# Branch gates and branch projections with tokens as output rows, in a two-block float32 kernel on one core

## The chip, the cores and the metric

The kernel runs on one core of a Trainium2 chip. TensorE, VectorE, ScalarE, GpSimd and the DMA queues each run their own program and meet at semaphores. The metric is the device time of one execution in microseconds, the median of several runs. All data are float32.

## What is computed

Two blocks of a sequence model over 256 tokens of width 1024. The change touches the middle of the first one:

```python
h = _rmsnorm(x, norm_mix_g[l])
z = h @ w_in[l]
(hq, hf, hi, hg, fq, fk, fv, ff, mq, gate_logits) = jnp.split(z, pts, axis=-1)
y_a = _hgrn2_mixer(...)      # 256 x 512
y_b = _fox_mixer(...)        # 256 x 512
y_c = _memory_mixer(...)     # 256 x 512
gates = jax.nn.sigmoid(gate_logits).reshape(B, T, N_BRANCH, D_MODEL)
merged = (gates[:, :, 0] * (y_a @ w_br_hgrn[l])
          + gates[:, :, 1] * (y_b @ w_br_fox[l])
          + gates[:, :, 2] * (y_c @ w_br_mem[l]))
x = x + merged @ w_out[l]
```

`gate_logits` is 256 x 3072; each branch projection is 512 x 1024, `w_out` 1024 x 1024. Feed-forward layers, a second attention block and more feed-forward layers follow.

## The kernel before

**Split precision.** Each matrix product is made of three float32r products on TensorE: high parts times high parts, high times low, low times high (`three`, L379). Weights come from memory in units of 128 x 2048, numbered in the order of use (`weight_plan`, `U[key]`). SyncE loads a unit into one of three raw buffers, ScalarE writes its high part `wh` (`hi_to`, L1039), VectorE subtracts it for the low part `wl` (`lo_to`, L1483). There are three slots of each, so unit j can't have its high part made before TensorE is done with unit j - 3 (`unit_end`). Both helpers are called by the other two programs at places written out by hand; `begin(key)` brings the parts up to two units ahead of the key's own. Each engine works strictly through its own list.

**Gates.** There are twelve gate units `("gate", u)` of 256 columns. `rows_out` (L421) makes one: the weights are the stationary operand, the turned activations `hT` (256 tokens wide) move, so the output has features as rows and tokens as columns: 2 x 8 x 3 matmuls of 256 columns. The PSUM banks are 0, 1, 6, 7 in turn for the first eight units, and 0 and 1 for the last four. VectorE multiplies the bank with the per-token norm factor into `BIGT` (`rows_scaled`, L1577). Between the units TensorE does the small products of the recurrent branch (`own_products`, `level_products`, `cross_products`, `hgrn_out`), for which VectorE and ScalarE prepare operands in the same loop over u (L1178, L1746). In iteration 7 ScalarE also places blocks into `Am` (L1187) and takes the sigmoid of the first eight gate units in four pieces (L1167); from iteration 8 an exponential is needed again (L1193), and each change between sigmoid and exponential loads a table.

**Branches.** `branch(bi, u, half, ...)` (L811) makes a quarter of a branch's projection: 24 matmuls of 256 columns, features as rows. VectorE multiplies it with its gate in `BIGT` (`gated`, L1854). GpSimd adds branches 0 and 1, VectorE adds branch 2 into `merged` and counts `mrg_all`. As `merged` has features as rows, ScalarE copies its high part (`merged_hi`) and VectorE its low part (`merged_lo`) straight from SBUF into `yTh`, `hTh`, `yTl`, `hTl`, where they are the stationary operand of the output projection (`stretch`, L881; units `("wo", 1, c, r)`). In VectorE's list the low part of the second of these units comes last, in two halves around `merged_lo(3)`.

**The form with tokens as rows** exists already: `toks_halves` (L475) takes two row halves of a 512-column weight unit; for each half r and each token half m, the activations are stationary and 512 columns of weights move, 12 matmuls into one bank per m. `hg`, `hi` and `mv` use it, and ScalarE evicts them with `half_scaled` (L1084), where the norm factor is a scale per partition.

Of the kernel before, what the change touches and what calls it, by code (L numbers as in the profile page):

```python
# [5 lines left out]
F32 = mybir.dt.float32  # L6
# [92 lines left out]
def weight_plan(I):  # L99
# [5 lines left out]
    plan += row_halves("hi", w_in, 1024)  # L105
    plan += [(("gate", u), cols(w_in, 4104 + 256 * u)) for u in range(12)]
    for u in range(2):
# [27 lines left out]
def build(nc, plan, I, out):  # L135
    ctx = ExitStack()
    with ctx:
# [79 lines left out]

        mrg_fox, mrg_all, m_hi, m_lo = (sem(n) for n in ("mrg_fox", "mrg_all", "m_hi", "m_lo"))

# [67 lines left out]
        def emptied(key):  # L287
            return ps_free[at[key][0]], 1

        def raw_ready(i):  # L290
# [75 lines left out]
        def pe_program(pe):  # L366
# [303 lines left out]

            for u in range(12):
                rows_out(("gate", u), WF if u < 8 else W, mid=cross_products if u == 10 else None)
                if u == 0:
                    own_products()
                elif u < 8:
                    level_products(u - 1)
                elif u == 10:
                    hgrn_out()

            b = T.take()  # L680
# [129 lines left out]

            def branch(bi, u, half, src, ready=None):  # L811
                i, b = U["br", bi, u], W.take()
                t = take(("br", bi, u, half), b)
                if half == 0:
                    weights(i)
                for m in range(2):
                    o = (2 * half + m) * 128
                    ins = three(t[:, m * 256:m * 256 + 256], weight_left(i, 512, o), right(src), EIGHT[:4], True, True,
                                ready if m == 0 else None)
                ins.then_inc(ps_full[b], 1)  # L820
                unit_end[i] = full(("br", bi, u, half))

# [48 lines left out]
            branch(1, 1, 1, hT_at)  # L871
            for u in range(2):
                for half in range(2):
                    branch(2, u, half, hT_c, (lambda k: free(("mo", k // 2)) if k % 2 == 0 else None) if (u, half) == (0, 0) else None)

# [28 lines left out]
            weights(U["wo", 1, 1, 0])  # L904
            pe.wait_ge(m_lo, 2)
            for m in range(2):
                stretch(("wo", 1, 1, 0), ts[m], m, EIGHT[:4])
            weights(U["wo", 1, 1, 1])
            for n, ks in enumerate(((4, 5), (6, 7))):
                pe.wait_ge(m_lo, 3 + n)  # L910
                for m in range(2):
                    stretch(("wo", 1, 1, 1), ts[m], m, ks)
# [122 lines left out]
        def act_program(act):  # L1035
# [119 lines left out]
            for m in range(2):  # L1155
                half_scaled(Iv, "hi", m, rs0)
            begin(("gate", 0))

# [5 lines left out]
            def gate_sigmoid(j):  # L1164
                g = BIGT[:, j * 1024:j * 1024 + 1024]
                act.wait_ge(*free(("gate", 2 * j + 1)))
                act.activation(g, g, ACT.Sigmoid).then_inc(gate_sig, 1)  # L1167

            def mem_squares(half):
                act.wait_ge(mem_in, 16)  # L1170
                for m in range(2):
                    if half or m:
                        act.wait_ge(mem_sq, 2 * half + m)
                    act.activation(Vm[:, 0:512], Hn[:, m * 1024 + half * 512:m * 1024 + half * 512 + 512], ACT.Square,
                                   accum_out=mstat[0][:, 2 * half + m:2 * half + m + 1]).then_inc(mem_sq, 1)

            level(0)
            for u in range(12):  # L1178
                begin(("gate", u))
                if u in (5, 6):  # L1180
                    mem_squares(u - 5)
                if 1 <= u <= 6:
                    level(u)
                elif u == 7:
                    act.wait_ge(*free(("lv", 4)))
                    for x in range(0, 128, 32):
                        act.activation(heads(Am[x:x + 32, :], 8)[:, :, x:x + 32], heads(Near[x:x + 32, :], 8),  # L1187
                                       ACT.Copy).then_inc(near_placed, 1)
                    for j in range(4):
                        gate_sigmoid(j)  # L1190
                elif u == 8:
                    act.wait_ge(ch_sub, 4)
                    act.activation(E1, E1, ACT.Exp).then_inc(ch_exp, 1)  # L1193
                elif u == 9:
                    act.wait_ge(*full("ax"))
                    act.wait_ge(lam_made, 1)
                    act.activation(Ax[:, :], bank[at["ax"][0]][:, :], ACT.Copy).then_inc(*emptied("ax"))
                elif u == 10:
                    for m in range(2):
                        act.wait_ge(*full(("ho", m)))  # L1200
                        act.activation(P[m][:, :], bank[6 + m][:, :], ACT.Square).then_inc(ho_sq, 1)
            for j in (4, 5):
                gate_sigmoid(j)
# [90 lines left out]
            def merged_hi(p):  # L1294
                h = (hTh if p > 1 else yTh)[:, p % 2 * 512:p % 2 * 512 + 512]
                act.wait_ge(mrg_all, p + 1)
                act.wait_ge(*unit_end[U["br", 1, 1] if p > 1 else U["br", 0, 1]])
                act.activation(h, merged[:, p * 512:p * 512 + 512], ACT.Copy).then_inc(m_hi, 1)

            begin(("br", 2, 0))  # L1300
            merged_hi(0)
            begin(("br", 2, 1))
            for p in (1, 2, 3):
                merged_hi(p)

# [17 lines left out]
            def toeplitz():  # L1323
                act.wait_ge(m_lo, 4)
                act.dma_start(BIGT[:, 0:4096], I["bias"]).then_inc(bias_in, 16)
                act.wait_ge(pv_done, 12)
                act.dma_start(times, I["times"]).then_inc(bias_in, 16)
# [151 lines left out]
        def dve_program(dve):  # L1479
# [223 lines left out]
            level_sub(0)  # L1703
            lo_to(U["gate", 0] + 2)
            level_mul(0)
# [40 lines left out]
            for u in range(12):  # L1746
                lo_to(U["gate", u] + (1 if u else 2))
                if 1 <= u < 7:
                    level_sub(u)
                rows_scaled(BIGT[:, u * 512:u * 512 + 512], ("gate", u))  # L1750
                if u == 0:
# [4 lines left out]
                elif u == 7:  # L1756
                    level_out(6)
                elif u == 8:
                    chunk_sub()
                    lo_to(U["gate", u] + 2)  # L1760
                    chunk_mul()
                elif u == 10:
                    hgrn_sums()
                if u:
                    lo_to(U["gate", u] + 2)
            hgrn_scaled()
# [190 lines left out]
            def merged_lo(p):  # L1957
                h, l = (x[:, p % 2 * 512:p % 2 * 512 + 512] for x in ((hTh, hTl) if p > 1 else (yTh, yTl)))
                dve.wait_ge(m_hi, p + 1)
                dve.tensor_tensor(l, merged[:, p * 512:p * 512 + 512], h.bitcast(F32), ALU.subtract).then_inc(m_lo, 1)  # L1960

            begin(("br", 2, 0))
            gated(2, 0, 0)
            gated(2, 0, 1)
            merged_lo(0)
            gated(2, 1, 0)
            merged_lo(1)
            merged_lo(2)
            gated(2, 1, 1)
            lo_half(U["br", 2, 1] + 2, 0)  # L1970
            merged_lo(3)
            lo_half(U["br", 2, 1] + 2, 1)

# [447 lines left out]
```

## Time and profile before

| | |
|---|---|
| median of 3 runs | 960.45 us (960.44 to 961.03) |
| profiled execution | 960.43 us, its span 958.6 us |
| TensorE matmul busy | 949.9 us, 99% |
| VectorE busy | 700.1 us, 73% |
| ScalarE busy | 515.7 us, 54% |
| GpSimd busy | 67.2 us, 7% |
| granted TensorE clock | 0.999 of full |

PE is TensorE, DVE is VectorE, ACT is ScalarE, POOL is GpSimd. The gates run from 54.5 to about 134.5 us of the span, the branches from 196.5 to 263.7, the output projection to about 286. Matmuls overlap in the records (one starts before the other's modelled end), so the time of one is read from start to start, not from its duration.

### The profile page before, as it was taken

What the parts mean: (1) busy time and instruction counts of PE and PEld (TensorE: products, weight loads), DVE (VectorE), ACT (ScalarE), POOL (GpSimd) and SP (SyncE); (2) the same over time, 40 slices, a digit from 0 to 9 for tenths busy, and PEclk for the clock granted to TensorE, in tenths of its full rate; (3) what the DMA queues carried; (4) which work ended last, traced back from release to release, by engine and by line L of the source; (5) the groups of instructions that cost most, each with busy time, mean ns of one, the idle gap of its engine ahead of it and who ended that gap; (6) DMA issues with size and microseconds to landing.
All of it is one profiled execution on the core that took longest, in us unless ns stands there. A gap on an engine that the chain in (4) does not pass through costs nothing.

```text
span 958.6 us, 15300 instructions
## 1 busy us (share of the span) xinstructions
PE 949.9 (99%) x6296; PEld 849.4 (89%) x6296; DVE 700.1 (73%) x1007; ACT 515.7 (54%) x653; POOL 67.2 (7%) x148
## 2 busy tenths in 40 slices
PE   9999999999999999999999999999999999999997
PEld 8899999998988888888888888889999888888886
DVE  5788767887777777888885766667678677666576
ACT  6665656555446555556663535446545555354454
POOL 1010223342200000000000000000002000000000
PEclk9999999999999999999999999999999999999999
DMA  9845444443464555555456464654533535646451
GB/s 352 312 150 177 137 171 153 157 159 129 153 254 168 199 192 203 176 191 185 169 203 219 155 226 149 222 200 142 181 133 132 195 135 199 227 149 218 173 176 45
DMA packets 25957, 174.16 MB, mean 182 GB/s; under 512 B 3360, under 2 KB 3616, under 8 KB 5792
## 3 DMA queue, kind: packets, MB, share of 16 engines
q1 hardware_dynamic: 25168, 170.11, 50.5%
q10 hardware_dynamic: 720, 3.07, 0.8%
q8 instruction: 50, 0.82, 0.3%
q14 instruction: 19, 0.16, 0.0%
HBM read 172.12 MB, written 1.05 MB: 181 GB/s over the span
## 4 chain that ended last, share of the span: by engine, by line
PE 96%; DVE 2%; ACT 1%; DMA 1%; issue 0%; SPq 0%; DVEq 0%; ACTq 0%
PE ps L385 53%; PE ps L394 24%; PE ps L398 13%; PE ps L500 1%; PE ps L711 1%; PE ps L742 1%; DVE wl L1489 1%; PE ps L726 1%; PE ps L775 1%; PE ps L641 1%; DMA BIGT<-in_first 1%; ACT wh L1047 0%; PE ps L789 0%; DVE P L2025 0%; PE ps L756 0%; PE ps L518 0%
## 5 line engine op out<-in xcount | busy, mean ns | idle before, releaser
L1489 DVE TENSOR_TENSOR wl<-raw,wh 128x2048 fp32r<-128x2048 f32 x152 | 347.6, 2288 | 30.4 <-ACT wh L1047 29.6
L1047 ACT ACTIVATE wh<-raw 128x2048 fp32r<-128x2048 f32 x155 | 295.9, 1910 | 27.9 <-PE ps L385 23.4
L394 PE MATMUL ps<-hT,wh 128*128 128x512 f32 x1056 | 248.3, 390 | 0.0
L394 PEld LDWEIGHTS ps<-hT,wh 128*128 128x128 f32 x1056 | 197.0, 188 | 40.8 <-DVE hT L1518 0.4
L385 PE MATMUL ps<-hT,wh 128*128 128x256 f32 (+1 forms) x912 | 168.2, 286 | 1.0 <-DVE wl L1597 0.6
L385 PEld LDWEIGHTS ps<-hT,wh 128*128 128x128 f32 (+1 forms) x912 | 140.6, 190 | 4.1 <-issue 1.5
L385 PE MATMUL ps<-wh,hT 128*128 128x256 f32 (+1 forms) x608 | 137.3, 315 | 0.0
L398 PEld LDWEIGHTS ps<-hT,wl 128*128 128x128 f32 x1056 | 132.4, 191 | 3.4
L1335 ACT ACTIVATE Am<-ps 128x512 f32<-128x512 f32 x66 | 39.1, 592 | 177.3 <-PE ps L398 175.5
L398 PE MATMUL ps<-hT,wl 128*128 128x256 f32 x1056 | 133.4, 283 | 0.0
L385 PE MATMUL ps<-hT,wl 128*128 128x256 f32 (+1 forms) x456 | 128.9, 283 | 0.0
L1574 DVE TENSOR_TENSOR PT<-ps,Am 128x256 f32<-128x256 f32 x132 | 49.7, 418 | 107.6 <-ACT Am L1335 107.2
L385 PE MATMUL ps<-wh,yTh 128*128 128x512 f32 (+1 forms) x298 | 116.4, 390 | 0.4 <-DVE yTl L2050 0.4
L385 PE MATMUL ps<-wl,yTh 128*128 128x512 f32 (+1 forms) x298 | 115.9, 389 | 0.0
L385 PE MATMUL ps<-wh,yTl 128*128 128x512 f32 (+1 forms) x298 | 115.6, 388 | 0.0
L385 PEld LDWEIGHTS ps<-wh,hT 128*128 128x128 f32 x608 | 101.0, 190 | 7.0 <-issue 0.8
L385 PE MATMUL ps<-wl,hT 128*128 128x256 f32 (+1 forms) x304 | 94.5, 311 | 0.0
L385 PEld LDWEIGHTS ps<-hT,wl 128*128 128x128 f32 (+1 forms) x456 | 86.4, 190 | 0.2
L385 PEld LDWEIGHTS ps<-wh,yTl 128*128 128x128 f32 x298 | 56.0, 188 | 11.8
L385 PEld LDWEIGHTS ps<-wh,yTh 128*128 128x128 f32 x298 | 56.1, 188 | 11.3 <-issue 0.8
L385 PEld LDWEIGHTS ps<-wl,yTh 128*128 128x128 f32 x298 | 56.1, 188 | 10.2
L385 PEld LDWEIGHTS ps<-wl,hT 128*128 128x128 f32 x304 | 57.9, 191 | 3.0
(257 smaller groups left out, 809.6 us busy)
## 6 DMA issues: line engine op xcount, KB each, us to landing
raw<-in_units SPq DMA_DIRECT2D x155, 1024.0 KB, 4.9
BIGT<-in_bias ACTq DMA_DIRECT2D x1, 2048.0 KB, 7.6
BIGT<-in_first SPq DMA_DIRECT2D x3, 512.0 KB, 6.3
raw<-in_units SPq DMA_DIRECT2D x2, 512.0 KB, 8.3
X<-in_x SPq DMA_DIRECT2D x1, 1024.0 KB, 15.4
Hn<-in_mem SPq DMA_DIRECT2D x1, 1024.0 KB, 10.2
XT<-in_mem_turned SPq DMA_DIRECT2D x1, 1024.0 KB, 12.2
out<-Hn SPq DMA_DIRECT2D x3, 256.0 KB, 2.1
```

The source lines that it names most:

```text
L385: ins = pe.matmul(o, l(k), r(k), start=first and k == ks[0] and j == 0, stop=last and k == ks[-1] and j == 2)
L394: pe.matmul(o, lh(k), hT_both(k), start=first and k == ks[0], stop=False)
L398: ins = pe.matmul(o[:, 256:512], ll(k), hT_at(k)[0], start=False, stop=last and k == ks[-1])
L500: ins = pe.transpose(t[:, q * 128:q * 128 + 128], src[:, m * n + k * 128:m * n + k * 128 + 128], ident)
L641: ins = pe.matmul(t[x:x + w, q * w + w - z:q * w + w], s[:, x:x + w], s[:, x + a:x + a + z], start=True, stop=True)
L711: ins = pe.matmul(t[:, x:z], l, r, start=True, stop=True)
L726: ins = pe.matmul(ts[j][:, x:z], q[ROW[j], c + m * 128:c + m * 128 + 128], k[ROW[j], c:c + z - x], start=True, stop=True)
L742: ins = pe.transpose(t[:, j * 128:j * 128 + 128], src[:, o:o + 128], ident)
L1047: act.activation(wh[j % NS][:, 0:n], raw[j % NR][:, 0:n], ACT.Copy).then_inc(w_hi, 1)
L1335: act.activation(v3(crossed_out(n)), t, ACT.Copy).then_inc(cross_made, 1)
L1489: dve.tensor_tensor(wl[j % NS][:, 0:n], raw[j % NR][:, 0:n], wh[j % NS][:, 0:n].bitcast(F32), ALU.subtract).then_inc(w_lo, 1)
L1574: dve.tensor_tensor(d[:, m, :], t[:, m, :], v3(crossed_out(n))[:, m, :], ALU.add).then_inc(*emptied((key, key + ("x",))[m]))
```

## The change

The twelve gate units of 256 columns become six of 512 in two row halves each, made by `toks_halves`; a branch quarter is now a token half times 512 weight columns. The first eight 256-column unit slots keep four banks, the last four two. The gates leave PSUM on ScalarE (`gate_out`), and VectorE's `rows_scaled` calls for them go. The sums `merged` now have tokens as rows; `merged_turn` turns them with four transposes for each of four pieces through banks 6 and 7, and `merged_hi` and `merged_lo` read these banks. VectorE's low part of the output units is called at other places: `begin(("br", 2, 1))` stands between the first and the second quarter of the third branch.

```diff
--- before.py
+++ after.py
@@ -103,7 +103,8 @@
     plan += [(("hq", u), cols(w_in, 256 * u)) for u in range(2)]
     plan += row_halves("hg", w_in, 1536)
     plan += row_halves("hi", w_in, 1024)
-    plan += [(("gate", u), cols(w_in, 4104 + 256 * u)) for u in range(12)]
+    for c in range(6):
+        plan += row_halves(("gate", c), w_in, 4104 + 512 * c)
     for u in range(2):
         plan += [((name, u), cols(w_in, a + 256 * u)) for name, a in (("fq", 2048), ("fk", 2560), ("fv", 3072))]
     plan += [(("mq", u), cols(w_in, 3592 + 256 * u)) for u in range(2)]
@@ -215,7 +216,7 @@
         bias_neg, bias_made = sem("bias_neg"), sem("bias_made")
         oa_sq, oa_sum, oa_done, sub_made = (sem(n) for n in ("oa_sq", "oa_sum", "oa_done", "sub_made"))
 
-        mrg_fox, mrg_all, m_hi, m_lo = (sem(n) for n in ("mrg_fox", "mrg_all", "m_hi", "m_lo"))
+        mrg_fox, mrg_all, m_hi = (sem(n) for n in ("mrg_fox", "mrg_all", "m_hi"))
 
         cross_made, up_made, act_made = (sem(n) for n in ("cross_made", "up_made", "act_made"))
         cv_in, cv_out, ff_act, ff_y, y_hi, y_lo = (sem(n) for n in ("cv_in", "cv_out", "ff_act", "ff_y", "y_hi", "y_lo"))
@@ -286,6 +287,9 @@
 
         def emptied(key):
             return ps_free[at[key][0]], 1
+
+        def gate_unit(u):
+            return U[("gate", u // 2), u % 2]
 
         def raw_ready(i):
             return raw_in[i % NR], 16 * (i // NR)
@@ -668,14 +672,19 @@
                         ins = pe.matmul(o, Am[:, (2 * h + m) * 128:(2 * h + m) * 128 + 128], iv[m], start=m == 0, stop=True)
                     ins.then_inc(ps_full[6 + m], 1)
 
-            for u in range(12):
-                rows_out(("gate", u), WF if u < 8 else W, mid=cross_products if u == 10 else None)
+            def levels_after(u):
                 if u == 0:
                     own_products()
                 elif u < 8:
                     level_products(u - 1)
                 elif u == 10:
                     hgrn_out()
+
+            for c in range(6):
+                mids = {(0, 1): lambda: levels_after(2 * c), (1, 1): lambda: levels_after(2 * c + 1)}
+                if c == 5:
+                    mids[0, 0] = cross_products
+                toks_halves(("gate", c), WF if c < 4 else W, mids)
 
             b = T.take()
             t = take("fcum", b)
@@ -808,17 +817,21 @@
                 pe.wait_ge(h_made, HEADS.index((name, u)) + 1)
                 turn(("ht", name, u), src, u, 512, False)
 
-            def branch(bi, u, half, src, ready=None):
+            def branch(bi, u, m, src, ready=None):
                 i, b = U["br", bi, u], W.take()
-                t = take(("br", bi, u, half), b)
-                if half == 0:
+                t = take(("br", bi, u, m), b)
+                if m == 0:
                     weights(i)
-                for m in range(2):
-                    o = (2 * half + m) * 128
-                    ins = three(t[:, m * 256:m * 256 + 256], weight_left(i, 512, o), right(src), EIGHT[:4], True, True,
-                                ready if m == 0 else None)
-                ins.then_inc(ps_full[b], 1)
-                unit_end[i] = full(("br", bi, u, half))
+                three(t[:, :], left(src, m), weight_wide(i, 0), EIGHT[:4], True, True, ready).then_inc(ps_full[b], 1)
+                unit_end[i] = full(("br", bi, u, m))
+
+            def merged_turn(p):
+                t = take(("mg", p), 6 + p % 2)
+                pe.wait_ge(mrg_all, p // 2 * 2 + 2)
+                for q in range(4):
+                    x = p // 2 * 1024 + q % 2 * 512 + (p % 2 * 2 + q // 2) * 128
+                    ins = pe.transpose(t[:, q * 128:q * 128 + 128], merged[:, x:x + 128], ident)
+                ins.then_inc(ps_full[6 + p % 2], 1)
 
             def hT_c(k):
                 return hT_at(k + 4)
@@ -869,9 +882,12 @@
             branch(1, 1, 0, hT_at)
             step(0, None, None, [11])
             branch(1, 1, 1, hT_at)
-            for u in range(2):
-                for half in range(2):
-                    branch(2, u, half, hT_c, (lambda k: free(("mo", k // 2)) if k % 2 == 0 else None) if (u, half) == (0, 0) else None)
+            branch(2, 0, 0, hT_c, lambda k: free(("mo", k // 2)) if k % 2 == 0 else None)
+            branch(2, 0, 1, hT_c)
+            branch(2, 1, 0, hT_c)
+            merged_turn(0)
+            merged_turn(1)
+            branch(2, 1, 1, hT_c)
 
 
             def begin_half(k, c, banks=T):
@@ -902,12 +918,15 @@
 
             ts = begin_half(1, 1)
             weights(U["wo", 1, 1, 0])
-            pe.wait_ge(m_lo, 2)
-            for m in range(2):
-                stretch(("wo", 1, 1, 0), ts[m], m, EIGHT[:4])
+            pe.wait_ge(*free(("mg", 0)))
+            pe.wait_ge(*free(("mg", 1)))
+            stretch(("wo", 1, 1, 0), ts[0], 0, EIGHT[:4])
+            merged_turn(2)
+            merged_turn(3)
+            stretch(("wo", 1, 1, 0), ts[1], 1, EIGHT[:4])
             weights(U["wo", 1, 1, 1])
             for n, ks in enumerate(((4, 5), (6, 7))):
-                pe.wait_ge(m_lo, 3 + n)
+                pe.wait_ge(*free(("mg", 2 + n)))
                 for m in range(2):
                     stretch(("wo", 1, 1, 1), ts[m], m, ks)
             second_half(1)
@@ -1154,7 +1173,7 @@
             begin(("hi", 1))
             for m in range(2):
                 half_scaled(Iv, "hi", m, rs0)
-            begin(("gate", 0))
+            hi_to(gate_unit(0) + 2)
 
 
             def level(n):
@@ -1163,7 +1182,8 @@
 
             def gate_sigmoid(j):
                 g = BIGT[:, j * 1024:j * 1024 + 1024]
-                act.wait_ge(*free(("gate", 2 * j + 1)))
+                for m in range(2):
+                    act.wait_ge(*free((("gate", j), m)))
                 act.activation(g, g, ACT.Sigmoid).then_inc(gate_sig, 1)
 
             def mem_squares(half):
@@ -1174,14 +1194,22 @@
                     act.activation(Vm[:, 0:512], Hn[:, m * 1024 + half * 512:m * 1024 + half * 512 + 512], ACT.Square,
                                    accum_out=mstat[0][:, 2 * half + m:2 * half + m + 1]).then_inc(mem_sq, 1)
 
+            def gate_out(u):
+                c, m = u // 2, u % 2
+                half_scaled(BIGT[:, c * 1024:c * 1024 + 1024], ("gate", c), m, rs0)
+
             level(0)
             for u in range(12):
-                begin(("gate", u))
+                hi_to(gate_unit(u) + 2)
+                if u >= 2 and u % 2 == 0 and u < 8:
+                    gate_out(u - 1)
                 if u in (5, 6):
                     mem_squares(u - 5)
                 if 1 <= u <= 6:
                     level(u)
                 elif u == 7:
+                    gate_out(6)
+                    gate_out(7)
                     act.wait_ge(*free(("lv", 4)))
                     for x in range(0, 128, 32):
                         act.activation(heads(Am[x:x + 32, :], 8)[:, :, x:x + 32], heads(Near[x:x + 32, :], 8),
@@ -1192,6 +1220,8 @@
                     act.wait_ge(ch_sub, 4)
                     act.activation(E1, E1, ACT.Exp).then_inc(ch_exp, 1)
                 elif u == 9:
+                    gate_out(8)
+                    gate_out(9)
                     act.wait_ge(*full("ax"))
                     act.wait_ge(lam_made, 1)
                     act.activation(Ax[:, :], bank[at["ax"][0]][:, :], ACT.Copy).then_inc(*emptied("ax"))
@@ -1199,6 +1229,9 @@
                     for m in range(2):
                         act.wait_ge(*full(("ho", m)))
                         act.activation(P[m][:, :], bank[6 + m][:, :], ACT.Square).then_inc(ho_sq, 1)
+                if u in (1, 3, 5, 11):
+                    gate_out(u - 1)
+            gate_out(11)
             for j in (4, 5):
                 gate_sigmoid(j)
 
@@ -1293,15 +1326,17 @@
 
             def merged_hi(p):
                 h = (hTh if p > 1 else yTh)[:, p % 2 * 512:p % 2 * 512 + 512]
-                act.wait_ge(mrg_all, p + 1)
+                act.wait_ge(*full(("mg", p)))
                 act.wait_ge(*unit_end[U["br", 1, 1] if p > 1 else U["br", 0, 1]])
-                act.activation(h, merged[:, p * 512:p * 512 + 512], ACT.Copy).then_inc(m_hi, 1)
+                act.activation(h, bank[6 + p % 2][:, :], ACT.Copy).then_inc(m_hi, 1)
 
             begin(("br", 2, 0))
+            begin(("br", 2, 1))
             merged_hi(0)
-            begin(("br", 2, 1))
-            for p in (1, 2, 3):
-                merged_hi(p)
+            merged_hi(1)
+            begin(("wo", 1, 1, 0))
+            merged_hi(2)
+            merged_hi(3)
 
 
             def project(k):
@@ -1321,7 +1356,7 @@
                 hi_to(U[key] + 3)
 
             def toeplitz():
-                act.wait_ge(m_lo, 4)
+                act.wait_ge(*free(("mg", 3)))
                 act.dma_start(BIGT[:, 0:4096], I["bias"]).then_inc(bias_in, 16)
                 act.wait_ge(pv_done, 12)
                 act.dma_start(times, I["times"]).then_inc(bias_in, 16)
@@ -1701,7 +1736,7 @@
             lo_to(U["hi", 1] + 2)
             dve.wait_ge(*seq.now())
             level_sub(0)
-            lo_to(U["gate", 0] + 2)
+            lo_to(gate_unit(0) + 2)
             level_mul(0)
             dve.wait_ge(masks_in, 16)
             dve.wait_ge(am_clear, 2)
@@ -1744,10 +1779,9 @@
                     dve.tensor_tensor(s, s, P[m][:, :], ALU.mult).then_inc(ya_made, 1)
 
             for u in range(12):
-                lo_to(U["gate", u] + (1 if u else 2))
+                lo_to(gate_unit(u) + (1 if u else 2))
                 if 1 <= u < 7:
                     level_sub(u)
-                rows_scaled(BIGT[:, u * 512:u * 512 + 512], ("gate", u))
                 if u == 0:
                     near_out("kq", 0, 0)
                 elif u < 7:
@@ -1757,12 +1791,12 @@
                     level_out(6)
                 elif u == 8:
                     chunk_sub()
-                    lo_to(U["gate", u] + 2)
+                    lo_to(gate_unit(u) + 2)
                     chunk_mul()
                 elif u == 10:
                     hgrn_sums()
                 if u:
-                    lo_to(U["gate", u] + 2)
+                    lo_to(gate_unit(u) + 2)
             hgrn_scaled()
 
             dve.wait_ge(*full("fcum"))
@@ -1957,19 +1991,19 @@
             def merged_lo(p):
                 h, l = (x[:, p % 2 * 512:p % 2 * 512 + 512] for x in ((hTh, hTl) if p > 1 else (yTh, yTl)))
                 dve.wait_ge(m_hi, p + 1)
-                dve.tensor_tensor(l, merged[:, p * 512:p * 512 + 512], h.bitcast(F32), ALU.subtract).then_inc(m_lo, 1)
+                dve.tensor_tensor(l, bank[6 + p % 2][:, :], h.bitcast(F32), ALU.subtract).then_inc(*emptied(("mg", p)))
 
             begin(("br", 2, 0))
             gated(2, 0, 0)
+            begin(("br", 2, 1))
             gated(2, 0, 1)
+            gated(2, 1, 0)
             merged_lo(0)
-            gated(2, 1, 0)
             merged_lo(1)
+            gated(2, 1, 1)
+            begin(("wo", 1, 1, 0))
             merged_lo(2)
-            gated(2, 1, 1)
-            lo_half(U["br", 2, 1] + 2, 0)
             merged_lo(3)
-            lo_half(U["br", 2, 1] + 2, 1)
 
 
             def project(k):
```

## Rows read from the trace of the kernel before

**Rows 1.** The page, busy time: engine, us (share of the span) xinstructions; one line.

```profile
PE 949.9 (99%) x6296; PEld 849.4 (89%) x6296; DVE 700.1 (73%) x1007; ACT 515.7 (54%) x653; POOL 67.2 (7%) x148
```

**Rows 2.** Waits of TensorE, waiter <- cause: us in total, times, longest; three of the four.

```profile
PE ps L578 <- POOL ones L2221: 1.0, 1, 1.0
PE ps L385 <- DVE wl L1597: 0.6, 1, 0.6
...
PE ps L385 <- DVE hT L1590: 0.3, 1, 0.3
```

**Rows 3.** Chain that ended last, in the gates: start us, us, what.

```profile
61.09 5.94 PE ps L385 x48
67.02 0.69 PE ps L641 x50
...
100.79 5.95 PE ps L385 x48
```

**Rows 4.** Timeline of TensorE, gate unit 8: start us, us, engine, line, operation.

```profile
107.74 0.50 PE L385 MATMUL ps<-hT,wh 128*128 128x256 f32 x2
...
108.44 0.28 PE L385 MATMUL ps<-hT,wl 128*128 128x256 f32 x1
...
108.80 0.28 PE L385 MATMUL ps<-hT,wl 128*128 128x256 f32 x1
```

**Rows 5.** Timeline of TensorE, units hi, tokens as rows, 512 columns.

```profile
47.91 0.39 PE L385 MATMUL ps<-wl,hT 128*128 128x512 f32 x1
...
53.35 0.39 PE L385 MATMUL ps<-wl,hT 128*128 128x512 f32 x1
```

**Rows 6.** Chain that ended last, transposes inside the output projection.

```profile
280.24 0.87 PE ps L500 x8
```

**Rows 7.** Timeline of VectorE: the eviction of gate unit 7.

```profile
106.78 0.69 DVE L1581 TENSOR_TENSOR BIGT<-ps,RB 128x512 f32<-128x512 f32 x1 [1.54 <-PE ps L385]
```

**Rows 8.** Timeline of ScalarE, 41 to 111 us; in brackets the idle time before.

```profile
41.56 0.67 ACT L1086 ACTIVATE Sg<-ps,sm 128x512 f32<-128x512 f32 x1
...
56.70 1.25 ACT L1086 ACTIVATE Iv<-ps,sm 128x512 f32<-128x512 f32 x2
...
86.14 1.06 ACT L1162 ACTIVATE HG<-HG 128x1024 f32<-128x1024 f32 x1 [3.76 <-DVE HG L1669]
87.11 1.90 ACT L1047 ACTIVATE wh<-raw 128x2048 fp32r<-128x2048 f32 x1
...
102.02 1.72 ACT L1187 ACTIVATE Am<-PT 32x256 f32<-32x256 f32 x4
103.75 1.28 ACT L1167 ACT_TABLE_LOAD   x1
105.05 3.90 ACT L1167 ACTIVATE BIGT<-BIGT 128x1024 f32<-128x1024 f32 x4
108.86 1.90 ACT L1047 ACTIVATE wh<-raw 128x2048 fp32r<-128x2048 f32 x1
```

**Rows 9.** Timeline of TensorE, the start of the third branch.

```profile
252.14 0.47 PE L385 MATMUL ps<-hT,wh 128*128 128x256 f32 x2
```

**Rows 10.** Timeline of ScalarE, the first output unit's high part.

```profile
252.24 1.92 ACT L1047 ACTIVATE wh<-raw 128x2048 fp32r<-128x2048 f32 x1 [2.27 <-PE ps L385]
```

**Rows 11.** Timeline of VectorE, its low part and the first two gated quarters.

```profile
254.19 2.52 DVE L1489 TENSOR_TENSOR wl<-raw,wh 128x2048 fp32r<-128x2048 f32 x1 [1.00 <-ACT wh L1047]
256.64 0.68 DVE L1860 TENSOR_TENSOR BIGT<-ps,BIGT 128x512 f32<-128x512 f32 x1
...
258.17 0.69 DVE L1860 TENSOR_TENSOR BIGT<-ps,BIGT 128x512 f32<-128x512 f32 x1
258.89 0.69 DVE L1864 TENSOR_TENSOR BIGT<-BIGT 128x512 f32<-128x512 f32 x1
```

**Rows 12.** Windows: us, width, busy of each engine, PEclk, DMA share, GB/s.

```profile
94.20:127.00 32.80, 32.80 (x307) 32.42 (x306) 22.63 (x34) 20.78 (x22) 4.89 (x15) 1.00 0.52 179
249.30:263.70 14.40, 14.40 (x121) 14.29 (x120) 12.21 (x14) 6.10 (x6) 4.54 (x2) 1.00 0.43 148
```

## The prediction

> **What bounds the kernel now.** I read the page first: TensorE is busy for 949.9 of the 958.6 us of the span, VectorE for 700.1 and ScalarE for 515.7 [rows 1]. The reader is to see two things there: nothing but TensorE can be the bound on average, and ScalarE and VectorE together still have little room to be late. Then the waits of TensorE: four of them, 2.3 us in all, the longest 1.0 [rows 2]. Then the chain of work in order of time, over the gates: it never leaves TensorE; each 256-column gate unit takes 5.94 us and the small products after it 0.69 [rows 3]. So the time is the sum of TensorE's own instructions, and a change is worth what it takes from or adds to that sum, plus each new wait of TensorE in full. The profiled execution took 960.43 us (span 958.6 and 1.8 around it), the median is 960.45, so I work on 960.45. Faster or slower by 0.2% is 1.92 us, about what a measurement of this kernel can tell from no change.
>
> **Part 1, the matmuls.** A matmul with 256 columns starts 120.0 ns after the one before it: from 108.44 to 108.80 us there are three, 0.36 us [rows 4]. One with 512 columns in the form that the gates will have (hT stationary, weights moving) takes 226.7: from 47.91 to 53.35 us there are 24 of them, 5.44 us [rows 5]. So a pair of the first costs 240.0, and one of the second saves 13.3 ns. The gates go from 12 x 48 = 576 matmuls to 288 and the branches from 288 to 144. The saving is 288 x 13.3 = 3.84 us in the gates and 144 x 13.3 = 1.92 in the branches, all of it on the path. The small products stand at the same number of places, and the restart after them is the same few hundredths to two tenths in both forms; I take nothing for it (bounds -0.1 to +0.1 at each of 9 places, since the rows show both signs of it only in part).
>
> These rows show a cost of 13.3 ns for each matmul beyond its 106.7 or 213.3 ns of columns at 2.4 GHz. The Trainium skill, page TensorE: Matmul & The Clock Gate, section "Wait — 56ns, not 53.3ns?", gives some 2.5 ns for a fixed cost of each warm matmul (measured in bf16). By that, half as many matmuls would save only 432 x 2.5 = 1.1 us, an estimate; the trace disagrees for this kernel's type.
>
> **Part 2, the turns.** The sums now have tokens as rows, so 16 transposes are added. Eight transposes between 512-column matmuls take 0.87 us from start to the next start [rows 6]; 16 cost 1.74 us, on the path. ScalarE and VectorE read the turned sums from PSUM instead of SBUF: four copies and four subtractions as before, of nearly the same size, off the path.
>
> **Part 3, the gates' eviction moves from VectorE to ScalarE.** VectorE loses 12 multiplications of 0.69 us [rows 7]; it is off the path, so this is worth nothing by itself. ScalarE gains 12 scaled copies out of PSUM of 0.67, one each 0.58 back to back (two took 1.25 together) [rows 8]. While the gates are below unit 7, ScalarE waits for VectorE for 2 to 4 us in each unit (one such wait stands as 3.76 [rows 8]), which covers its 0.6. It isn't covered behind unit 7. There ScalarE's order becomes: wait for the end of unit 7, evict gate 7, four copies into Am (1.73 us), a table load (1.30), four sigmoids (3.81), the high part of unit 10's weights (1.91), a table load (1.28), the exponential (0.97), the high part of unit 11 (1.90), and only then evict gate 8. Before, the copies, the table and three of the four sigmoids ran during unit 7, since no eviction stood ahead of them: the Am copies began at 102.02, the high part of unit 10 at 108.86 [rows 8]. Bank 0, which holds gate 8 (the first half of the fifth 512-column gate), is the one that the sixth gate must start in, as the last two gates have only banks 0 and 1.
>
> I count from the end of unit 7's matmuls, 106.62: its last one starts 48 x 0.12 = 5.76 and a restart of 0.1 after 100.79 [rows 3], and the products start behind it. ScalarE follows a finish by 0.16 (VectorE's eviction starts at 106.78 [rows 7]). So 0.16 + 0.58 + 1.73 + 1.30 + 3.81 + 1.91 + 1.28 + 0.97 + 1.90 = 13.6, and the eviction's 0.67 ends at 14.3. TensorE does level products until 1.12 (107.74 [rows 4]) and then units 8 and 9 in 10.88, with 0.1 for the restart: it wants the bank at 12.1. It waits 2.2 us. Bounds: 0, if ScalarE is earlier by as much (the table loads hoisted), and 3.0, if the eviction and the Am copies each take their full latency. VectorE's low part of unit 10 ends at 9.5 + 2.3 = 11.8, just before 12.1, so that wait is hidden by the other. The chunk products of VectorE end at 13.5 and are wanted at about 17. Behind the blocked eviction on ScalarE stands the eviction of gate 9, wanted 2.7 + 0.9 later; it is done by then. After the gates, two sigmoids and a weight copy are done some 0.7 us before the first query head is full; no wait there.
>
> **Part 4, the third branch.** I count from A = 252.14, where the third branch's first matmul starts behind the second branch's last [rows 9]. Before: ScalarE makes the high part of the first output weights at 252.24, VectorE its low part at 254.19, then VectorE gates and adds the first quarter (256.64) and the second (258.17, 258.89) [rows 10, 11]. The low part of the second output unit comes last, behind all four quarters. The change puts it between the first and the second gated quarter on VectorE. Its high part can't begin before the slot's owner, the first unit of the third branch, is finished, which is after the second quarter's matmuls, at A + 2 x 2.72 = 5.44. From there: 2.05 to the start of the low part (from 252.14 to 254.19, signals and high part), 2.2 for the low part, 1.41 for gating and adding the second quarter (from 258.17 to the end of 258.89 + 0.69), 0.05 for the signal: A + 11.15. TensorE has only the third quarter in between (A + 8.16), then stands at the first turn, which needs both quarters. It waits 3.0 us. Bounds: 2.4 (every step back to back at its pitch) and 3.6 (the low part at the 2.45 to 2.52 us that the one at 254.19 took [rows 11]). Queued behind that turn are the fourth quarter and the whole output projection, so the wait counts in full.
>
> What follows it: turns 0 and 1 end at 12.0, the fourth quarter at 14.7, the first output stretch at 17.5, turns 2 and 3 at 18.3, the second stretch at 21.1. VectorE has the low parts of sums 0 and 1 at about 13.6 (wanted 14.7) and of sums 2 and 3 at 19.8 and 20.4 (wanted 21.1 and later). Both are in time by 1 us. Earlier branches: their evictions and copies have room of 1 us and more in the rows that I read. The low parts of the memory values are made just as the third branch begins, by the two steps before 252.6 on VectorE; I take nothing, bound 0.2.
>
> **Sum.** -3.84 - 1.92 + 1.74 + 2.2 + 3.0 = +1.2 us: 961.6. The change gives back in two waits, and in its turns, what it gains in half as many matmuls.
>
> **Rivals.**
> 1. One of the two waits isn't there. For it: ScalarE is idle for much of the gates, and my chain of nine steps behind unit 7 is long; against it: each step is a row, and the order on each queue is fixed in the program. Without the gates' wait 959.4, without the branch's 958.6. Chance 0.13.
> 2. Neither is there: the change is worth its arithmetic, 960.45 - 3.84 - 1.92 + 1.74 = 956.4. It needs both chains to be misread. Chance 0.04.
> 3. Slower, a third wait: the turned second half of the sums. VectorE makes a whole low part (2.28) for the next weights before the low parts of sums 2 and 3, behind ScalarE's high part. If these slip by more than the 1.3 and 0.7 us of room, TensorE waits in the middle of the output projection. With one more operation of that size in the way the wait is 2.28 - 0.7 = 1.6: 963.2. Chance 0.11.
> 4. Slower, the clock: TensorE's granted clock is 1.00, which is 2.4 GHz, in every window of these stages [rows 12], and its waits until now are 1.0 us at most [rows 2]. No row shows it after a wait of 3 us. If it fell to 1.2 GHz there, each unit of 24 matmuls run so would take 10.88 instead of 5.44: about +5.4 for one, 967.0. Chance 0.06. The Trainium skill, same page, section "HAM oscillation — how this bites in real kernels", says that idle gaps of TensorE in the middle of a kernel bring the slower clock back; no run yet shows it here.
> 5. The 512-column form saves only what the page's fixed cost would give: +1.2 + 4.7 = 966.3. The rows speak against it, as the gates' very form is among them [rows 5]. Chance 0.01.
>
> **How the numbers follow.** The forecast, both waits within 0.8 us of my sum, has 0.65; of it 0.06 lies above 962.37. Slower: 0.06 + 0.11 + 0.06 + 0.01 = 0.24. Faster: rival 2, and of rival 1 the 0.05 in which the branch's wait is missing and more: 0.09. Same: the rest, 0.67. The range goes from the case without the gates' wait with a little more, 958.9, to the third wait with the upper bounds, 963.6; below lie about 0.08, above about 0.1.
>
> **What would show it.** In the profile after: 24-matmul stretches of 5.44 us in the gates and 2.72 for a branch quarter; a wait of TensorE of about 2.2 us for ScalarE's eviction about three units before the gates' end, and one of about 3.0 for VectorE's addition before the first turn of the sums; 0.87 for eight turns; TensorE's busy time 4.0 us less. The prediction is wrong if either wait is missing or twice as long, if a third appears, or if the granted clock falls.

## The result and the profile after

The changed kernel takes 964.73 us (median of 9, 962.83 to 967.87) beside 960.84 for the kernel before (9 runs on the same chips, 959.95 to 963.96). The ratio is 1.0046, its interval 1.0037 to 1.0056. It is slower by 0.46%, some 4 us, where I had forecast 961.6, no change that can be told, with 963.6 as the upper end.

The waits of TensorE in the profiled execution of the changed kernel (967.87 us, span 966.0), which answer [rows 2]; columns: waiter, cause, us in total, times, longest:

```profile
PE ps L833 <- DVE BIGT L1898: 3.0, 1, 3.0
PE ps L389 <- ACT BIGT L1105: 2.1, 1, 2.1
PE ps L389 <- DVE hT L1625: 1.8, 1, 1.8
PE ps L582 <- POOL ones L2255: 1.0, 1, 1.0
```

The first two are the waits of the prediction: 3.0 us for VectorE's addition before the first turn (forecast 3.0), and 2.1 us for ScalarE's eviction before the sixth gate (forecast 2.2). The third is at the start of the kernel, where ScalarE waits 2.29 us for the input `in_first` instead of 0.76; this late input costs some 1.6 us. It comes and goes: a profile of the kernel before with edits only in its later stages (the run with four operations on GpSimd, below) has it with 1.4 us, the profile of the changed kernel without its two waits has it with 0.2. The change doesn't touch this code.

The page's busy time of the kernel after, for [rows 1]:

```profile
PE 951.1 (98%) x5880; PEld 829.9 (86%) x5880; DVE 692.3 (72%) x994; ACT 522.9 (54%) x665; POOL 67.8 (7%) x148
```

There are 416 matmuls fewer (432 less, 16 turns more), yet TensorE's busy time rose by 1.2 us. Windows of the kernel after around the two waits, in the columns of [rows 12]; the number to read is the granted clock, the third from the end:

```profile
119.00:122.00 3.00, 1.62 (x6) 1.38 (x7) 2.89 (x4) 1.82 (x3) 0.00 (x0) 0.92 0.85 325
122.00:125.00 3.00, 3.00 (x9) 2.33 (x8) 0.00 (x0) 0.00 (x0) 0.00 (x0) 0.51 0.72 202
125.00:128.00 3.00, 3.00 (x19) 2.58 (x18) 0.00 (x0) 2.12 (x2) 0.00 (x0) 1.00 0.36 150
263.00:265.00 2.00, 0.00 (x0) 0.00 (x0) 1.97 (x4) 0.00 (x0) 0.00 (x0) 0.97 0.28 33
265.00:268.00 3.00, 2.88 (x11) 2.72 (x12) 2.23 (x4) 1.19 (x2) 0.00 (x0) 0.50 0.78 328
268.00:271.00 3.00, 3.00 (x14) 2.40 (x14) 0.93 (x2) 0.51 (x1) 0.00 (x0) 0.95 0.00 0
```

After each of the two waits the clock is at 0.50, that is 1.2 GHz, for some 3.4 us, and then at 2.4 GHz again. I call such a stretch a fall of the clock. The first fall begins 1 us after TensorE has resumed, the second in the wait itself. The timeline of TensorE at the gates' wait shows both, the start times of 512-column matmuls before and in the fall:

```profile
120.38 0.47 PE L389 MATMUL ps<-wh,hT 128*128 128x512 f32 x1 [2.07 <-ACT BIGT L1105]
120.68 0.40 PE L389 MATMUL ps<-wl,hT 128*128 128x512 f32 x1
120.92 0.62 PE L389 MATMUL ps<-wh,hT 128*128 128x512 f32 x2
121.37 0.48 PE L389 MATMUL ps<-wl,hT 128*128 128x512 f32 x1
121.66 1.05 PE L389 MATMUL ps<-wh,hT 128*128 128x512 f32 x2
122.51 0.63 PE L389 MATMUL ps<-wl,hT 128*128 128x512 f32 x1
```

From 121.66 to 122.51 two matmuls take 0.85 us; from 120.92 to 121.37 two took 0.45. The chain shows the same for the turns, beside 0.87 for eight in [rows 6], and for the quarter and the output stretch behind them (24 matmuls, 5.44 at full clock):

```profile
265.12 1.94 PE ps L833 x8
267.06 6.12 PE ps L389 x24
273.17 0.87 PE ps L833 x8
```

### The profile page after: what moved, and what is told of

Read it like the earlier page. It is cut to its first block, busy times and chain, and to the rows that moved or that the text cites. A ratio compares the mean times of both kernels' runs of the same rounds, so it can differ in the third digit from the quotient of the medians.

```text
span 966.0 us, 14471 instructions
## 1 busy us (share of the span) xinstructions
PE 951.1 (98%) x5880; PEld 829.9 (86%) x5880; DVE 692.3 (72%) x994; ACT 522.9 (54%) x665; POOL 67.8 (7%) x148
## 4 chain that ended last, share of the span: by engine, by line
PE 94%; DVE 2%; ACT 2%; issue 1%; DMA 1%; SPq 0%; DVEq 0%; ACTq 0%
PE ps L389 50%; PE ps L398 24%; PE ps L402 12%; PE ps L504 1%; PE ps L720 1%; PE ps L751 1%; DVE wl L1524 1%; ACT wh L1066 1%; PE ps L735 1%; DMA BIGT<-in_first 1%; PE ps L784 1%; PE ps L645 0%; PE ps L798 0%; DVE P L2059 0%; PE ps L765 0%
## 5 line engine op out<-in xcount | busy, mean ns | idle before, releaser
L389 PE MATMUL ps<-wh,hT 128*128 128x256 f32 (+1 forms) x864 | 222.7, 342 | 2.1 <-ACT BIGT L1105 2.1
L389 PEld LDWEIGHTS ps<-wh,hT 128*128 128x128 f32 x864 | 150.1, 191 | 20.3 <-issue 3.7
L389 PE MATMUL ps<-wl,hT 128*128 128x256 f32 (+1 forms) x432 | 145.2, 336 | 0.0
L389 PE MATMUL ps<-wh,yTh 128*128 128x512 f32 (+1 forms) x314 | 123.0, 392 | 0.4 <-DVE yTl L2084 0.4
L389 PE MATMUL ps<-wh,yTl 128*128 128x512 f32 (+1 forms) x314 | 121.9, 388 | 0.0
L389 PEld LDWEIGHTS ps<-wl,hT 128*128 128x128 f32 x432 | 82.5, 191 | 7.7
L389 PE MATMUL ps<-hT,wh 128*128 128x256 f32 (+1 forms) x400 | 73.9, 286 | 2.1 <-DVE hT L1625 1.8
L389 PEld LDWEIGHTS ps<-hT,wh 128*128 128x128 f32 (+1 forms) x400 | 60.9, 187 | 4.7 <-DVE hT L1625 2.0
L389 PE MATMUL ps<-hT,wl 128*128 128x256 f32 (+1 forms) x200 | 56.5, 283 | 0.0
L1261 ACT ACTIVATE P<-ps,sm 128x256 f32<-128x256 f32 (+1 forms) x56 | 23.5, 425 | 39.4 <-DVE sm L1874 22.2
```

Source lines behind the costliest of these rows:

```text
L389: ins = pe.matmul(o, l(k), r(k), start=first and k == ks[0] and j == 0, stop=last and k == ks[-1] and j == 2)
L1261: act.activation(P[i % 2][:, x:z], t[:, x:z], ACT.Exp, bias=mn[:, c], scale=-1.0, accum_out=den[:, c]).then_inc(*(emptied(key) if m else s ...
```

## The experiments

The theory after the result: the change is its arithmetic, plus the two waits, plus a stretch at 1.2 GHz behind each, worth 3.4 x 0.5 = 1.7 us. The rivals: the 512-column form itself loses more; or the fall of the clock is chance of one profile, and a wait costs its length only.

**Both waits taken away.** The sigmoids leave ScalarE's iteration 7, two go behind the copy of `Ax` in iteration 9, one into iteration 11 and the rest behind the loop, and the low part of the second output unit goes behind the fourth quarter:

```diff
-                    for j in range(4):
-                        gate_sigmoid(j)
...
+                    for j in range(2):
+                        gate_sigmoid(j)
...
+                if u == 11:
+                    gate_sigmoid(2)
...
-            for j in (4, 5):
+            for j in (3, 4, 5):
                 gate_sigmoid(j)
...
             gated(2, 0, 0)
-            begin(("br", 2, 1))
             gated(2, 0, 1)
...
             gated(2, 1, 1)
-            begin(("wo", 1, 1, 0))
+            begin(("br", 2, 1))
             merged_lo(2)
```

> The changed kernel without its two waits: four sigmoids of the gates are taken later on ScalarE, and VectorE makes the low part of the second output unit behind the fourth quarter. Theory (arithmetic of the matmuls plus two waits, each with a stretch at the lower clock): the waits go, the granted clock stays at 1.00 in the middle of the kernel, and what is left is -3.84 - 1.92 + 1.74 = -4.0 us against the kernel before: 956.8, ratio 0.9958, and a spread of runs like that of before. Rival (the 512-column form itself costs more than the rows say, so that the loss is in the matmuls): still slower than 960.

Measured: 957.63 us (957.38 to 959.33), ratio 0.9964 (0.9951 to 0.9976): faster than both kernels. Between the lowest executions of the two (957.38 and 960.19) lie 2.8 us, 0.29%; the ratio gives more, since the executions of the kernel before spread further upwards. The busy times and the clock of the whole stretch:

```profile
90.00:275.00 185.00, 184.77 (x1230) 162.48 (x1229) 136.40 (x213) 108.50 (x159) 52.73 (x111) 1.00 0.45 160
```

Neither of the two waits and no fall of the clock is left between 90 and 275 us. The rival of the costly form is refuted. But the gain is 2.8 us in this profile (span 955.8 beside 958.6, with the same start), not the 4.0 of my arithmetic. The chain tells where the 1.2 us went; lines of this kernel, for [rows 3] and from the later stages:

```profile
92.59 5.67 PE ps L389 x24
...
131.89 17.27 PE ps L389 x144
...
213.54 0.66 PE ps L504 x4
...
245.36 2.77 PE ps L389 x12
248.13 0.04 issue
248.17 8.42 PE ps L389 x36
...
256.59 0.88 PE ps L833 x8
...
277.42 0.87 PE ps L504 x8
```

And two of the kernel before at the same steps, the first query head and the turn of the memory keys:

```profile
135.27 17.27 PE ps L385 x144
...
217.12 0.44 PE ps L500 x4
```

A gate unit between small products went from 5.94 to 5.67, which is 0.27 instead of 0.32, and a branch quarter from 2.87 to 2.77 or 2.73, which is 0.10 to 0.14 instead of 0.16. Wherever TensorE comes back from small products in these stages, the unit behind them gains a few hundredths of a microsecond less than the arithmetic gave; I put this down to the restart. The end of the gates is earlier by 3.38 us instead of 3.84 (131.89 beside 135.27 for the first query head). To the third branch's start (248.17 beside 252.14 in [rows 9]) another 0.6 are gained instead of 1.28; 0.22 of what is missing is a single turn of the memory keys that stands as 0.66 us where it was 0.44. From there to the turns of the next norm (277.42 here, 280.24 in [rows 6]) 29.3 us go by, 28.1 before: +1.2, with +1.1 expected.

**One wait at a time.** These are the two halves of the edit above, each alone.

> Only the branch's wait is taken away (the low part of the second output unit behind the fourth quarter); the gates' wait of 2.1 us stays. Theory: 956.8 + 2.2 = 959.0 without a fall of the clock and 960.7 with one of 3.4 us at half rate; the median lies between. Rival (a wait costs its own length and the clock is chance of this one profile): 959.0 in every run.

> Only the gates' wait is taken away (sigmoids later); the branch's wait of 3.0 us stays. Theory: 956.8 + 3.0 = 959.8 without and 961.5 with a fall of the clock. Rival (a wait costs its own length): 959.8 in every run.

With the branch's wait gone and the gates' left: 961.58 us (median of 11; ratio 1.0000, 0.9988 to 1.0013). The executions lie in groups: four at 959.7 to 959.9, three at 961.5 to 962.0, four at 963.0 to 963.5. The lowest group is 957.5 + 2.1, without a fall. The next is 1.8 us above it, which can be one fall or the late input: two of its three have a mean granted clock of 0.996, lower than in any of the 26 executions of the kernel before (0.997 to 1.000), and so a fall; the third has 0.998 and stays open. The last group is another 1.5 us on; the profiled execution, 963.04 us, is in it and has both the fall and the late input. With the gates' wait gone and the branch's left: 963.48 us (median of 10; ratio 1.0021, 1.0012 to 1.0031), none below 962.2, where 957.5 + 3.0 = 960.5 would be without a fall. So behind the 2.1 us the clock fell in some executions but not in all. Behind the 3.0 us the times say that it fell in all ten of this kernel, though only one of them was profiled. In that profile the clock stayed down for twice as long, 0.62 on average over 9 us:

```profile
258.00:267.00 9.00, 6.16 (x19) 5.26 (x20) 5.34 (x7) 1.19 (x2) 0.00 (x0) 0.62 0.34 122
```

That is 9 x 0.38 = 3.4 us lost, double of the 1.7. The rival by which a wait costs only its own length is refuted.

The nine executions of the changed kernel show that even its two waits together can pass without a fall. One took 962.83 us, which is 957.6 + 2.1 + 3.0. Another, of 964.49 us, has a mean granted clock of 0.999; one fall alone takes 1.7 of 963 us, or 0.0018, from the mean, and 0.999 leaves room for 0.0015 at most. So it had none, and its time is that of the late input. The other seven have 0.996 or 0.997.

**The waits filled with work.** TensorE does matmuls in them that nobody reads:

```diff
                 if c == 5:
                     mids[0, 0] = cross_products
+                    pe.wait_ge(ps_free[6], tiles.free[6])
+                    for _ in range(9):
+                        pe.matmul(bank[6][:, :], hTh[:, 0:128], hTh[:, 0:512], start=True, stop=True)
...
                 t = take(("mg", p), 6 + p % 2)
+                if p == 0:
+                    for _ in range(13):
+                        pe.matmul(t[:, :], hTh[:, 0:128], hTh[:, 0:512], start=True, stop=True)
```

> The changed kernel with its two waits, but TensorE works in them: 9 matmuls of 512 columns before the sixth gate into bank 6 (2.04 us) and 13 before the first turn (2.95 us), whose results nobody reads. Theory: the same time goes to the waits, but the clock stays at 1.00, so 956.8 + 2.2 + 3.0 = 962.0, with all runs within about 1 us, against 964.7 of the changed kernel. Rival (what the changed kernel loses beyond its two waits isn't the clock after idle time): 964 to 965 and the wide spread remain.

Measured: 963.18 us (median of 11; nine at 962.7 to 963.7, two at 964.6 and 964.9); ratio 1.0022 (1.0013 to 1.0031). Nearly the same time stands between the same steps (9 and 13 matmuls at 226.7 ns are 2.04 and 2.95 us), but the clock stays up:

```profile
116.00:128.00 12.00, 11.96 (x62) 9.90 (x61) 6.00 (x10) 7.40 (x7) 0.00 (x0) 1.00 0.50 175
258.00:270.00 12.00, 12.00 (x57) 9.71 (x57) 8.27 (x11) 4.92 (x4) 0.00 (x0) 1.00 0.45 171
```

With the arithmetic put right, 957.6 + 2.1 + 3.0 = 962.7 is expected and 963.2 measured; the 0.5 us between them weren't looked into. A kernel with useless work in its waits is 1.5 us faster by the medians than the one that stands idle in them, and the intervals of the two ratios don't overlap. The mean clock of all eleven executions is 0.998 or 0.999. So it is TensorE's idle time that brings the lower clock, not the stage.

**Waits by themselves, in the kernel before.** In the first two feed-forward layers TensorE stops eight times for a chain of small operations on GpSimd, whose number is 1, 4, 8 or 11 (here four):

```diff
                             ins = down_part(f, j - 1, n)
+                            if n == 2 and f < 2 and j in (2, 4, 6, 8):
+                                ins.then_inc(pe_stops, 1)
+                                pe.wait_ge(pool_goes, 4 * f + j // 2)
...
+            for stop in range(8):
+                pool.wait_ge(pe_stops, stop + 1)
+                for r in range(4):
+                    x = scratch_p[0][:, 0:8]
+                    pool.wait_ge(*seq.now())
+                    pool.tensor_scalar(x, x, 1.0, None, ALU.mult).then_inc(*(seq.next() if r < 3 else (pool_goes, 1)))
```

> The kernel before, in which TensorE is made to wait eight times in the first two feed-forward layers for four small operations of GpSimd (4 x 0.28 us and the signals, about 1.3 us each); TensorE is the bound there, so each wait costs its length: about +10. Theory (idle time of TensorE brings the lower clock back, and a wait of some 2 us does so in some places, one of 3 us nearly always, each for 1.7 us): at 1.3 us none or few of eight fall, so 961 + 10 = 971 and a clock of 1.00 in the feed-forward layers. Rival (any wait costs the clock): 971 + 8 x 1.7 = 984.

> The same with eight operations of GpSimd at each of the eight places: waits of about 2.4 us, 19 in all. Theory: some of the eight bring the lower clock, other ones in other executions: 961 + 19 = 980 and some 3 to 6 times 1.7, 985 to 990. Rival (the two places in the changed kernel are special, since the stages there are): no fall of the clock, 980.

> The same with eleven operations of GpSimd: waits of about 3.3 us, 26 in all. Theory: nearly all eight bring the lower clock for some 3.4 us: 961 + 26 + 8 x 1.7 = 1001. Rival (as above): no fall of the clock, 987.

> The kernel before with eight waits of TensorE for one operation of GpSimd each. From the two lengths of the run with four and with eight operations (1.97 and 3.23 us where GpSimd ran at its usual pace) one operation gives 1.97 - 3 x 0.315 = 1.0 us, 8 us in all. Theory (only a wait that leaves a long enough hole brings the lower clock; 2 of 4 did at 1.97 us): none of eight falls, 961 + 8 = 969. Rival (each wait has a share of falls whatever its length): a few of eight fall, 972 and more.

Measured: 1000.19, 1020.23 and 1028.7 us with 4, 8 and 11 operations (4 runs each), and 969.15 with one. In the first three the waits came out longer than I had aimed for, as GpSimd's chains took 1.8 to 7.7 us, so the totals of these expectations are void. The single waits are what counts, each with the clock behind it. Those of the run with four operations, four waits of 1.97 us and four of 4.09, in windows that begin at most 2.4 us before the end of the wait (the granted clock is again the third number from the end):

```profile
332.00:342.00 10.00, 8.03 (x36) 6.35 (x35) 8.04 (x9) 6.19 (x6) 1.58 (x4) 1.00 0.52 165
368.00:378.00 10.00, 8.29 (x36) 6.86 (x37) 7.42 (x8) 6.19 (x6) 1.41 (x4) 1.00 0.49 179
404.00:414.00 10.00, 8.89 (x32) 7.22 (x33) 8.28 (x8) 5.04 (x5) 0.91 (x2) 0.83 0.55 197
441.00:451.00 10.00, 8.91 (x32) 7.20 (x33) 7.14 (x7) 4.94 (x5) 0.91 (x2) 0.83 0.61 223
533.00:543.00 10.00, 8.70 (x31) 7.03 (x32) 3.13 (x3) 1.91 (x1) 1.08 (x3) 0.83 0.42 143
573.00:583.00 10.00, 9.59 (x36) 7.85 (x37) 2.29 (x1) 1.92 (x1) 0.28 (x2) 0.83 0.42 136
611.00:621.00 10.00, 8.67 (x28) 6.98 (x29) 3.17 (x3) 1.91 (x1) 1.11 (x3) 0.68 0.37 118
651.00:661.00 10.00, 8.83 (x26) 7.03 (x27) 3.00 (x3) 1.91 (x1) 0.95 (x3) 0.66 0.39 120
```

Two of the four waits of 1.97 us brought no fall and two brought one of 1.7 us (10 x 0.17). All four of 4.09 us brought one: two of 1.7 and two of 3.2 to 3.4. In the runs with 8 and 11 operations there were two waits of 3.23 us, of which one brought a fall, and fourteen of 4.6 to 7.9, which all did. These falls are longer: fourteen of the fifteen cost 3.4 us each (20 x 0.17), and the one behind a wait of 7.08 us costs 5.2 (20 x 0.26), as these two windows show, the first from the run with 8 operations, the second from the run with 11:

```profile
365.00:385.00 20.00, 16.77 (x72) 13.72 (x71) 10.32 (x12) 6.80 (x8) 2.45 (x8) 0.83 0.45 157
...
455.00:475.00 20.00, 12.92 (x52) 10.65 (x52) 7.79 (x9) 5.42 (x5) 6.05 (x11) 0.74 0.43 152
```

With one operation the waits are 0.58 and 0.97 us, eight of them, and the clock doesn't fall:

```profile
PE ps L386 <- POOL sm L2302: 6.2, 8, 1.0
...
300.00:700.00 400.00, 393.39 (x2189) 340.95 (x2188) 290.79 (x374) 210.83 (x235) 4.67 (x8) 1.00 0.53 182
```

Here each stop costs its own length, about (969.15 - 960.5) / 8 = 1.1 us, of which 0.58 or 0.97 is the wait and the rest is put down to drain and restart (960.5 is the kernel before without the late input). So neither of the rivals holds as it was put: the places in the changed kernel aren't special, and a short wait is only as long as it is.

## Why the prediction was wrong

**Right: what bounds the kernel, and the two waits.** The order on each queue and the durations of [rows 7 to 11] gave 2.2 and 3.0 us; the trace has 2.1 and 3.0. The bank that gate 8 held, and the low part that VectorE had to make before the second quarter, were the causes; taking them away took the waits away. The 0.87 us for eight turns came as read from [rows 6] wherever the clock was up.

**Mis-sized: the arithmetic of the matmuls.** This step of the sum took 13.3 ns for every second matmul, 5.76 us in all, and nothing for the restarts. Its bound for these was too narrow, since it counted 9 places; there are about twenty. Arithmetic and turns together were worth -2.8 us, not -4.0. This alone gives 960.45 - 2.8 + 5.1 = 962.8, still inside the range. A small wait of 0.3 us in the third branch's first matmuls, as VectorE makes the low part of the memory values, is part of it; I had given it 0.2 at most.

**The step that failed: the clock.** It stood as rival 4, slower, with a chance of 0.06, and in the sum it stood at nothing. Its price there, one unit at half rate or 5.4 us, was three times too high. What the runs showed in its place: behind a wait of 2 us a fall comes in some cases and not in others (two of four in one trace), behind the 3.0 us in all ten executions of the kernel that has it alone, by their times, and one fall costs 1.7 us, at times twice that. The changed kernel has both waits, so most of its executions have one or two falls: 962.8 + 1.7 = 964.5, and 966.2 with both, and 1.6 more where the input is late. Three of the nine executions lie at 964.4 to 964.7 with a mean clock of 0.997, the median of 964.73 among them; one is at 966.27, three are at 967.1 to 967.9, and all four of these have 0.996; two had no fall, as told above. The profiled one adds up too, as spans: 958.6 - 2.8 + 2.1 + 3.0 + 1.7 + 1.7 + 1.6 for the late input = 965.9, and it is 966.0. I had argued from the absence of a fall behind waits of up to 1.0 us [rows 2], which says nothing of one of 3 us. The Trainium skill, page TensorE: Matmul & The Clock Gate, section "HAM oscillation — how this bites in real kernels", says that idle gaps bring the slower clock back in the middle of a kernel. These runs agree: the granted clock was 0.50 for 3.4 us behind the waits of 2.1 and of 3.0 us. This rival would have deserved the larger chance.

**Rivals.** Missing waits (rivals 1 and 2) and the third wait behind the turned second half (3) are refuted by the waits of the profile after. The smaller gain by the fixed cost that the prediction took from the Trainium skill (page TensorE: Matmul & The Clock Gate, section "Wait — 56ns, not 53.3ns?"), rival 5, is refuted by the kernel without waits: by it, with the turns, that kernel would be slower than before (-1.1 + 1.7), and it is faster by 0.36%.

**What stays open:** why a wait of 3.23 us brought no fall once when shorter ones did, why two executions of the changed kernel had none, and when a fall lasts 3.4 us, when twice and when three times as long. How many of the single executions had a fall isn't shown, as only one of each kernel was profiled; their times and mean clocks are what speaks for it. Why the input at the start lands late wasn't looked into.

## What to carry to other kernels

When a change puts a new wait on a TensorE that was never idle, price it as its length plus the clock behind it. In these runs that was nothing more at 1 us, 1.7 us or nothing at 2 us, mostly 1.7 or 3.4 us and now and then nothing at 3 us, and 1.7 to 5.2 us at 4 us and above. Before a wait is put down as the price of a change, look at what stands ahead of its releaser on that engine's list: here two reorderings, of sigmoids that nobody needed yet and of a low part that wasn't due, turned 0.46% slower into 0.36% faster. Where matmuls are joined into wider ones, count the places at which TensorE comes back from small work; each took a little of the gain here.

## What the runs showed of the hardware

The lower clock can begin after TensorE has resumed: 1 us into the work behind the gates' wait, in the middle of dense matmuls. And useless matmuls in a wait kept the clock at 2.4 GHz and made the kernel 1.5 us faster (963.18 beside 964.73).
